# Two heads of index scores and latent queries issued together into two PSUM banks, transposes with one bank

## The reference, cut to what matters

```
q_a, c_kv, q_idx, k_idx, w_idx, q_b, k_b, v_b, f_in = split(x @ w_in)
q_lat = einsum('bshd,hrd->bshr', q_a, w_uk) * 64**-0.5       # latent queries: per head 64 -> 128
# per block of 128 queries:
idx   = einsum('bthd,bsd->bths', q_idx, k_idx)               # 8 heads, contraction over 64
score = einsum('bth,bths->bts', w_idx, relu(idx))            # summed over heads
sel   = top_k(masked score, 128)                             # which keys the latent attention may see
la    = q_lat . c_sel + position bias ; oa = softmax(la) @ c_sel
lb    = q_b . k_b + forget terms      ; ob = softmax(lb) @ v_b
```

## Time and profile before

| | us |
|---|---|
| median of 3 runs | 1915.85 (1915.56 to 1916.55) |
| the profiled execution | 1915.55 |
| its span, first to last instruction | 1913.5 |
| even mixer, from the first F step to the first product behind it | 708.8 to 951.5 |
| PE busy in the span | 1871.7 (98%) |
| DVE, ACT, POOL busy | 928.1, 727.5, 386.2 |
| mean granted TensorE clock | 0.993 of full speed |

### The profile page before, as it was taken

How to read it: one execution, slowest core, us unless ns; L and a number is a source line. 1 busy time by engine, 2 the same in 40 slices (tenths; PEclk the granted TensorE clock), 3 DMA queues, 4 the chain that set the end, 5 groups by cost and what they waited for, 6 DMA issues and landing times.

```text
span 1913.5 us, 23337 instructions
## 1 busy us (share of the span) xinstructions
PE 1871.7 (98%) x9766; PEld 1543.6 (81%) x9766; DVE 928.1 (49%) x1501; ACT 727.5 (38%) x1223; POOL 386.2 (20%) x224
## 2 busy tenths in 40 slices
PE   7999988999999999999999999999989999999998
PEld 6788977888888888777788888888768898888886
DVE  5675544322322234776555555523543366556334
ACT  5664434322322243556734334321323244344211
POOL 1433433111110034211031111100254421111000
PEclk9999989999999999999999999999999999999999
DMA  5211032232233232110022322332322322322321
GB/s 198 69 53 67 7 120 81 88 103 95 90 109 110 80 136 69 67 42 26 23 82 95 101 98 89 118 113 78 110 88 87 112 78 99 108 91 91 119 99 66
DMA packets 28764, 170.01 MB, mean 89 GB/s; under 512 B 3386, under 2 KB 5602, under 8 KB 10866
## 3 DMA queue, kind: packets, MB, share of 16 engines
q1 hardware_dynamic: 28660, 168.53, 25.4%
HBM read 166.37 MB, written 2.11 MB: 88 GB/s over the span
## 4 chain that ended last, share of the span: by engine, by line
PE 93%; DVE 3%; ACT 2%; POOL 1%; issue 0%; DMA 0%; SPq 0%; ACTq 0%; DVEq 0%
PE ps L572 27%; PE ps L573 27%; PE ps L574 27%; PE ps L1112 2%; PE ps L1040 1%; PE ps L1075 1%; PE ps L1079 1%; PE ps L1097 1%; POOL wL L2494 1%; PE ps L652 1%; ACT wH L1281 1%; PE ps L702 1%; PE ps L856 0%; PE ps L865 0%; DVE hL L1819 0%; PE ps L1051 0%
## 5 line engine op out<-in xcount | busy, mean ns | idle before, releaser
L572 PE MATMUL ps<-hH,wH 128*128 128x512 f32 (+1 forms) x1568 | 603.3, 385 | 5.4 <-POOL wL L2494 1.9
L574 PE MATMUL ps<-hH,wL 128*128 128x512 f32 (+1 forms) x1568 | 591.1, 377 | 0.0
L573 PE MATMUL ps<-hL,wH 128*128 128x512 f32 (+1 forms) x1568 | 591.0, 377 | 0.0
L1812 DVE TENSOR_TENSOR wL<-raw,wH 128x1024 fp32r<-128x1024 f32 (+1 forms) x196 | 240.3, 1265 | 331.5 <-ACT wH L1281 331.5
L1281 ACT ACTIVATE wH<-raw 128x1024 fp32r<-128x1024 f32 (+2 forms) x298 | 290.2, 1023 | 282.5 <-PE ps L574 282.5
L2494 POOL TENSOR_TENSOR wL<-raw,wH 128x1024 fp32r<-128x1024 f32 (+2 forms) x102 | 246.4, 2438 | 689.8 <-ACT wH L1281 689.8
L572 PEld LDWEIGHTS ps<-hH,wH 128*128 128x128 f32 x1568 | 296.1, 189 | 66.6 <-issue 5.5
L574 PEld LDWEIGHTS ps<-hH,wL 128*128 128x128 f32 x1568 | 295.8, 189 | 54.4
L573 PEld LDWEIGHTS ps<-hL,wH 128*128 128x128 f32 x1568 | 296.1, 189 | 52.3 <-issue 1.4
L572 PE MATMUL ps<-wH,aH 128*128 128x512 f32 x528 | 209.0, 396 | 0.0
L574 PE MATMUL ps<-wH,aL 128*128 128x512 f32 x528 | 208.8, 395 | 0.0
(11 more groups left out here) (370 smaller groups left out, 1918.8 us busy)
## 6 DMA issues: line engine op xcount, KB each, us to landing
raw<-in_wbig SPq DMA_DIRECT2D x139, 1024.0 KB, 4.8
rows<-in_rows SPq DMA_DIRECT2D x12, 512.0 KB, 5.8
x<-in_x SPq DMA_DIRECT2D x8, 512.0 KB, 5.7
raw<-in_wbig SPq DMA_DIRECT2D x8, 512.0 KB, 3.6
out<-x SPq DMA_DIRECT2D x4, 512.0 KB, 2.6
near<-u_scratch SPq DMA_DIRECT2D x1, 1024.0 KB, 7.3
raw<-in_wbig SPq DMA_DIRECT2D x1, 1000.0 KB, 8.1
raw<-in_wbig SPq DMA_DIRECT2D x1, 600.0 KB, 10.7
```

Of the source, the lines that this page charges most:

```text
L572: e.matmul(o, hi, m_hi, start=first, stop=False)
L573: e.matmul(o, hi, m_lo, start=False, stop=False)
L574: return e.matmul(o, lo, m_hi, start=False, stop=end)
L1812: e.tensor_tensor(wL[r][:, cs], raw[r][:, cs], wH[r][:, cs].bitcast(F32), ALU.subtract).then_inc(*low_dve.one(c, h))
```

## The change

The index scores of heads 2hp and 2hp+1 are issued in one step, the even head into bank 7 and the odd head into bank 5, after a wait for both banks. The second step of each pair issues nothing on PE. The latent queries are paired the same way. ACT reads from bank 7 or 5 by the parity of the head, at the same steps as before. Since bank 5 is taken, the transposes of all units use bank 4. The string of the order is another one, with the same counts (156 F, 96 I, 192 A).

```diff
-    return ("FFFFFIFFFFFFFFFFFFFFFFFFFFFIFFFFFFFFFFFFFFFFIFFFFFFFIFIFFIFIFIFIFIFIFFFIFFIIFFIIIIFFFFIIFFFFIFIIFAFIFFFIIIFFIFFIAFAFFAIA"
...
+    return ("FFFFIFFFFFFFFFFFFFIFFFFFFFFFFFFFFIFFFFFFFFFFFFFFFFFIFFIFIIFIIFFIIFFIFFIIFFIIFIIIIFFFFIFFFFFFFFIAIIAFFFAIFFFIAFIIIAFIAFA"
...
-                    for h in range(8):
-                        s = slice(64 * (h % 2), 64 * (h % 2) + 64)
-                        clear(7)
+                    for hp in range(4):
                         w.wait_ge(*even.act.at("ki"))
-                        e.matmul(ps[7][:, 0:n], qiT[h // 2][s, 128 * i:128 * i + 128], kiT[s, 0:n], start=True, stop=True).then_inc(*idx.pe.one("s", i, h))
-                        bank[7] = [idx.act.at("relu", i, h)]
+                        clear(7, 5)
+                        for h in (2 * hp, 2 * hp + 1):
+                            s, b = halves[h % 2], PAIR[h % 2]
+                            e.matmul(ps[b][:, 0:n], qiT[hp][s, 128 * i:128 * i + 128], kiT[s, 0:n], start=True, stop=True).then_inc(*idx.pe.one("s", i, h))
+                            bank[b] = [idx.act.at("relu", i, h)]
+                        yield
                         yield
...
-                    r = slice(64 * (h % 2), 64 * (h % 2) + 64)
-                    clear(7)
-                    w.wait_ge(*D["wuk"].at())
-                    w.wait_ge(*even.act.at("qa", h // 2))
-                    e.matmul(ps[7][:, :], wuk[r, h // 2, :], qaT[h // 2][r, :], start=True, stop=True).then_inc(*lat.pe.one("ql", h))
-                    bank[7] = [lat.act.at("ql", h)]
+                    if h % 2 == 0:
+                        w.wait_ge(*D["wuk"].at())
+                        w.wait_ge(*even.act.at("qa", h // 2))
+                        clear(7, 5)
+                        for g, r in enumerate(halves):
+                            e.matmul(ps[PAIR[g]][:, :], wuk[r, h // 2, :], qaT[h // 2][r, :], start=True, stop=True).then_inc(*lat.pe.one("ql", h + g))
+                            bank[PAIR[g]] = [lat.act.at("ql", h + g)]
                     yield
...
-                        i, b = (n + 1) % 4, 4 + (n + 1) % 2
+                        i, b = (n + 1) % 4, 4
                         clear(b)
...
+        PAIR = (7, 5)
...
-                        e.activation(rel[h % 2][:, 0:n], ps[7][:, 0:n], ACT.Relu).then_inc(*idx.act.one("relu", i, h))
+                        e.activation(rel[h % 2][:, 0:n], ps[PAIR[h % 2]][:, 0:n], ACT.Relu).then_inc(*idx.act.one("relu", i, h))
...
-                    e.activation(ql[h % 2][:, :], ps[7][:, :], ACT.Copy, scale=0.125).then_inc(*lat.act.one("ql", h))
+                    e.activation(ql[h % 2][:, :], ps[PAIR[h % 2]][:, :], ACT.Copy, scale=0.125).then_inc(*lat.act.one("ql", h))
...
-                        e.activation(Pt[u % 2][:, 0:wd], ps[4 + u % 2][:, 0:wd], ACT.Copy).then_inc(*unit.act.one("turn", u))
+                        e.activation(Pt[u % 2][:, 0:wd], ps[4][:, 0:wd], ACT.Copy).then_inc(*unit.act.one("turn", u))
```

More of the change, by code:

```diff
@@ L249, in even_order @@
 def even_order():
-    return ("FFFFFIFFFFFFFFFFFFFFFFFFFFFIFFFFFFFFFFFFFFFFIFFFFFFFIFIFFIFIFIFIFIFIFFFIFFIIFFIIIIFFFFIIFFFFIFIIFAFIFFFIIIFFIFFIAFAFFAIA"
-            "AAAIAAFAIAAIAFAFIAIFFIAIFAAAAFFAAIAAFIAAIFAAIAAIAIFAIFAAAFAIFIFAIFFFFIIAAIAIAFFIAFAFAAIFFAAIAAIAFFAIFFIAFIAFAIAAFAFIAFAI"
-            "AFAIAIIAAFAAIFIFFAIAAFFIAAAFFFFFAAFFIAIAAAFIAAFIAIFFIFAAIAAAFIIAAFAFIAFAAAAIAAIAFIAAIFAIAAFIAAAAAIAAAAAIAAAFAAAAIAAAAAFI"
-            "AFAAFAIAAAAIAAAAAAAFAFIAAAAFAIAAAAAIAAAAIAAAAAAAAAAIAAAAAAAAAAIAAAAAAAFAAAAFAAAFAAFA")
+    return ("FFFFIFFFFFFFFFFFFFIFFFFFFFFFFFFFFFIFFFFFFFFFFFFFFFFFIFFIFIIFIIFFIIFFIFFIIFFIIFIIIIFFFFIFFFFFFFFIAIIAFFFAIFFFIAFIIIAFIAFA"
+            "AIFFIIAFIAAIAAAFAIFIAFIAIAAAFFFIAIAFAIFIFAFAAFIFAAFFAAFAAIIAIFAAAIFFAFAIAAFAAFIAIAIIFFAAFAAIFIAIIFFIAAAAAAFAFIIAAAIAAAAI"
+            "FFIFFFAFIAFAFFIAIAFAIFAAIFAAFAAIFAAAAAIFAFFFIIAAIAAIFIFFIIFAAFIAAFAFFAAAAIFFIAAAAIAAIAIAIFAAAFAAAFAAAIAIAAAAIFIAAAFAAAAA"
+            "AAAAIAAIAAAAAAAAFAAAAAFAAAAIIAAAAFAAFAAAAAAIAAAIAAAAFAAAIAAAAAIAAAAFAAAAAAAAAAAFAAFA")
 def odd_order():
```

## The result

The changed kernel takes 1900.3 us in the median of 4 runs (1899.25 to 1900.92), the kernel before 1915.7 us on the same chip (4 runs, 1913.69 to 1916.55). The ratio is 0.9921, with a 95% interval of 0.9909 to 0.9934. When it was measured once more beside another kernel, the ratio was 0.9920 (0.9906 to 0.9933).

The account below looks back on a forecast made before the run. PE was taken to bound the even mixer, issuing without a stop. -17.1 + 0.9 + 0.7 + 0.6 = -14.9 us from 1915.55 gave 1900.65 profiled, about 1901.0 us median; own range 1898.5 to 1905, with the rivals to 1909.

Parts of the forecast that it names:

- The pairs: Index scores and latent queries in the even mixer: a pair costs what one head cost, saving 17.1 us.
- Full overlap from L725: Earlier trace at L725: eight 256-column instructions on opposite halves take 1.06 us, as four would; so paired heads overlap fully.
- No overlap: Even mixer pairs: rival that only one entering and leaving is saved per pair; 11.2 us dearer, 1912.2 us; chance 0.06.
- The order: New string in the even mixer: products charged by their neighbours cost 0.9 us more, bounds 0 and +2 us.
- nothing is to be had or lost from the clock: Even mixer: clock at its full level, 2.4 GHz, over the whole stretch, so no gain or loss from it.
- Waits for two banks: PE before each pair in the even mixer, waiting for both `relu`s of the pair before: 0.7 us, bounds 0 and 9.
- The one bank: Transposes waiting for ACT's copy of the unit before: 0.6 us, mainly unit 62 late by 0.45 us; bounds 0 and 6.
- the other hand-overs keep 1.1 us or more: Single transpose bank: apart from unit 61 to 62, each hand-over has at least 1.1 us to spare.
- Outside the stage, nothing: Everything before and behind the even mixer stays unchanged.
- the signs that the prediction named: Even mixer: stage 227 to 229 us instead of 242.7, PE's waits 1 to 3 us more, 512-column pair about 1.05 us.
- Rivals 1 to 4: 1 one-instruction overlap 1906.6 (0.08); 2 no overlap 1912.2 (0.06); 3 draining bound 1909.3 (0.08); 4 transpose bank 1921 (0.04).
- partial overlap: Even mixer pairs: rival that the halves overlap by only one instruction; 5.6 us dearer, 1906.6 us; chance 0.08.

## Why the prediction was right

The forecast was 1901.0 us, measured 1900.3.

- *The pairs, -17.1 us.* Right in mechanism: a pair costs what a head cost, in each of the three widths (0.63, 0.85 and 1.06 us from its start to the next matmul, where a head took 0.63, 0.84 and 1.05). The size was measured only together with the order: the stage shrank by 16.3 us, against -17.1 + 0.9 = -16.2 before any waits. Set against the 1.0 us of the one bank (below) and the 0.4 us of `ota` that went away, pairs and order together gave about 16.9 us, an estimate; so the order cost less than 0.9 or the pairs gave more than 17.1.
- *Full overlap from L725.* Right: the earlier trace rows carried over from four and four instructions to two and two: 0.64 us for a 256-column pair leaves no room for a third slot of 0.215, and the odd head's first instruction starts 0.01 us behind the even head's first and 0.31 us ahead of its second. So the rule of the Trainium skill (page "TensorE: Matmul & The Clock Gate", section "Part 3: Packing small matmuls — row/col tiling") that matmuls start and end in program order does not hold for these pairs, and the measurement decides.
- *No overlap, 11.2 us dearer.* Measured with both heads on one half: 11.0 in the stage.
- *The order, +0.9 us.* No run bears the tally out. Under pairs, with the stall taken away, the new string's stage was 1.7 us shorter than the old one's, and not longer. What the tally could not see is that the string had a task. Pairs under the old string would have taken 1905.8, because behind a wait of 0.9 us for DVE the clock was at half for 6.8 us. That nothing is to be had or lost from the clock held for this string and not for the old one, and nothing in the prediction told the two apart: in that it was lucky. I priced the change as a whole, so the forecast did not suffer, but "the order is worth nothing", my expectation for that run, was wrong by 5 us.
- *Waits for two banks, +0.7 us.* Mis-sized: no wait of a pair for `rel` or `ql` is listed. The gaps in the trace are as I counted them, but the pairs need less than I took: the second `relu` ends 1.82 us after the start of a 384-column pair (I had 2.1) and 2.25 us after that of a 512-column pair (I had 2.5), against closest gaps of 2.03 and 2.58 us.

```profile
782.36 0.92 PE L1041 MATMUL ps<-kiT,qiT 64*128 64x384 f32 x4
783.31 0.87 ACT L1653 ACTIVATE rel<-ps 128x384 f32<-128x384 f32 x2 [1.80 <-PE ps L1041]
784.39 0.59 PE L1041 MATMUL ps<-kiT,qiT 64*128 64x384 f32 x2
```

- *The one bank, +0.6 us.* The place was right: unit 62's transposes show 0.30 us of idle time for unit 61's copy, and by the distance of starts (0.58 instead of 0.11) they are 0.47 us late, where I had 0.45. But "the other hand-overs keep 1.1 us or more" was wrong. Those of units 63 and 43 were released by the copy too, 0.3 and 0.2 us late, so the one bank costs about 1.0 us by this estimate. Alone, under the old string, it cost 1.0 as well. Copies and transposes as in the earlier trace rows, units 61 to 63:

```profile
930.87 0.33 PE L1115 MATMUL ps<-va,Pt 128*128 128x64 f32 x2
931.07 0.38 ACT L1687 ACTIVATE Pt<-ps 128x256 f32<-128x256 f32 x1 [0.23 <-PE ps L1100]
931.51 0.55 PE L1100 MATMUL ps<-ident,rows 128*128 128x128 f32 x3 [0.30 <-ACT Pt L1687]
932.49 0.47 ACT L1687 ACTIVATE Pt<-ps 128x384 f32<-128x384 f32 x1
933.02 0.66 PE L1100 MATMUL ps<-ident,rows 128*128 128x128 f32 x4
```

- *Outside the stage, nothing.* The stage gave 1.4 us more than I forecast, and the longer stretches at half clock took 1.7 us in the profiled execution. The two misses cancel, so the total is closer than the terms: that the median came within 0.7 us is in part luck. Of the signs that the prediction named, the stage (226.4 us) fell just under its 227 to 229, and the listed waits did not grow by 1 to 3 us but stayed as they were.

Rivals 1 to 4 are all out: 1.06 us for a wide pair, where partial overlap asked for about 1.5 and none for 1.9, no listed wait of the scores (L1041), and about 1 us late for `Pt` instead of 21.

## What to carry to other kernels

Two fp32 matmuls with contraction 64 on opposite halves of the partitions, back to back into different banks, cost the time of one here, and a group of that kind elsewhere in the same trace told it beforehand. When TensorE gets faster, look at what its old slowness was hiding. A stall of about 1 us among sparse matmuls cost 4.6 us here, because the clock fell behind it (gone when the stall was), and moving two steps of other work ahead of it brought that back. A list of waits can be silent on a microsecond that sits in many short hand-overs; the distances between starts show it. The order and the pairing belong together: the order made for pairs made single heads 0.44% slower.

## What the runs showed of the hardware

- Overlap of the halves survives a semaphore update and a fulfilled wait between the two heads. In the changed kernel's trace four instructions of a 256-column pair hold PE for 0.64 us from the first start to the next matmul, on one half for 1.06 us.
- The granted clock fell to half three times where the kernel it was compared with stayed at full, each time behind a stretch in which PE had been idle for part of it: busy 2.31 of 3.50 us, 5.31 of 6.00 us and 2.69 of 4.00 us. It then stayed there for 6.8, 3.4 and 3.4 us although PE was busy without a gap. Where the idle time was removed at two of these places, the fall was gone. What decides between a fall and none was not measured: the changed kernel's 0.30 us of idle time near the end drew none.
- The same matmuls in the same order at the start of the odd mixer were at half clock for about 7 us in some executions and for 10.2 us in others, 1.3 us of time. The runs of one kernel scatter with the mean granted clock: the kernel before took 1913.5 us at 0.995 and 1916.8 us at 0.992 on one chip.
